# First sequence's difference-attention value pages issued by SyncE instead of GpSimd

## The chip, the core and the metric

The kernel runs on one core of a Trainium2 chip. The time is that of one execution on the device in microseconds (us), and the median of three runs of the kernel before is 1414.11 us. The core has five engines that run their own instruction streams and meet at semaphores: TensorE (PE in the profile), VectorE (DVE), ScalarE (ACT), GpSimd (POOL) and SyncE (SP). SyncE and GpSimd issue nearly all transfers of this kernel.

## The reference, cut to what matters

One decoder layer works on a prompt of 256 tokens and on 8 sequences of 8 new tokens each, all with one set of weights. The part in question is the attention of the 8 new-token sequences over 1024 cached positions. It has a sparse mixer and a difference mixer:

```python
def diff_attention(q, k, v, qp, kp, lam):
    ...
        s = jnp.einsum('bqhcd,bkhcd->bhcqk', q_b, k) * SCALE
        p = masked_softmax(s, kp[None, :] <= qp_b[:, None])
        p_diff = p[:, :, 0] - lam * p[:, :, 1]
        return jnp.einsum('bhqk,bkhe->bqhe', p_diff.astype(v.dtype), v)
```

The cached keys and values lie in pages of 128 positions, picked by a page table. Each sequence has 8 pages of difference keys (`cache_diff_k`, 256 KB each), 8 of difference values (`cache_diff_v`, 256 KB each), 8 of compressed keys and values (`cache_cmp_kv`, 128 KB each) and 8 of selected ones (`cache_sel_kv`, 128 KB each). After the attention come two projections and a mixture of 32 experts.

## The kernel before, in words

The cached attention runs in four turns, each for a pair of sequences, b = 0 and b = 1 (`PAIRS_OF_SEQ` is 4). The first three turns are a hardware loop on each engine and the fourth is written out. Every engine follows an order written out by hand, and semaphores join them. No scheduler decides anything.

TensorE's turn, in the order of the code (`turn` in `pe_attention`):

- `kd0` to `kd7` (L611) transpose the key pages of this turn's b = 1 out of `dk_raw`, spread among the matmuls of `hidden` (L625). Then come the difference scores (L634, L639).
- A second run of `hidden` follows, with `pd0` to `pd2` and the groups of selected and window keys among it, then the scores of the sparse mixer (L749 to L757).
- `dif_values(0)` multiplies the b = 0 probabilities with `dv_raw[0]` (L687, L689), then a small product (L766), then `dif_values(1)` does the same with `dv_raw[1]`. Each adds one to the semaphore `l_pv`. These two are called D0 and D1 below.
- `nk0` and `nk1` (L611) then transpose the first key pages of the next turn's b = 0. Before `nk0` TensorE waits until four pages (0 to 3) have landed in `dk_raw`, and before `nk4` until pages 4 to 7 have. `ps0`, `ps1`, a product (L776), `pw` and `pm` lie between, and `nk2` to `nk7` follow.
- The values of the sparse mixer (L701 to L708) and the next turn's b = 0 scores (L634) end the turn.

There is one `dk_raw` for all keys, so it is filled twice per turn: with the pages of b = 0 of turn i during turn i - 1, as `kd0` to `kd7` of that turn free it, and with those of b = 1 as `nk0` to `nk7` free it. `dv_raw` has a buffer for each b.

SyncE issues, for each turn, the keys of b = 0 (`dk_pages(i, 0)`, which waits for `kd3` and `kd7` of turn i - 1), the keys of b = 1 (`dk_pages(i, 1)`, which waits for `nk3` and `nk7`), and the selected pages (`sel_pages`, which wait for the last values of the turn). A read of the page table (`pages_of`, L465) stands at the head of each pass.

GpSimd issues the compressed pages (`cmp_pages`, L482, which wait for VectorE's `cmp_turned`), copies queries (L545), and issues the value pages of both sequences (`values_in`, L539). Those of b = 0 wait until D0 of the turn before has read the old ones, and those of b = 1 until D1 of the turn before and `pd2` of the present turn are over.

An instruction that waits holds up all that stand behind it on its engine.

Of the kernel before, what the change touches and what calls it, by code (L numbers as in the profile page):

```python
# [30 lines left out]
NPAGE = PAST // PAGE  # L31
RUN = 4
# [119 lines left out]
def build(nc, io, const_a, at_a, const_b, at_b):  # L152
    ctx = ExitStack()
    with ctx:
# [4 lines left out]
        def at(off, *dims):  # L159

            n = int(np.prod(dims))
            v = arena[:, off:off + n]
            if len(dims) == 2:
                return v.rearrange("p (a b) -> p a b", b=dims[1])
            if len(dims) == 3:
                return v.rearrange("p (a b c) -> p a b c", b=dims[1], c=dims[2])
            if len(dims) == 4:
                return v.rearrange("p (a b c d) -> p a b c d", b=dims[1], c=dims[2], d=dims[3])
            return v
# [9 lines left out]
        dv_raw = [at(6144, NPAGE, 512), at(33792, NPAGE, 512)]  # L179
# [102 lines left out]
        pv_full, nsa_out, dif_out = sem("pv_full"), sem("nsa_out"), sem("dif_out")  # L282
# [16 lines left out]
        STAGES = (("sel", 0), ("win", 0), ("cmp", 0), ("dif", 0), ("dif", 1), ("sel", 1), ("win", 1), ("cmp", 1))  # L299
# [90 lines left out]
        dv_in = [sem(f"dv_in{k}") for k in range(4)]  # L390
        l_tp, l_out = sem("l_tp"), [sem("l_out_act"), sem("l_out_dve")]
# [5 lines left out]
        l_pv, l_osm = sem("l_pv"), sem("l_osm")  # L397
# [4 lines left out]
        def past(eng, s, n):  # L402


            eng.wait_ge(s, n + 1)
# [14 lines left out]
        SCORES, EXPS, VALUES = 2, 4, 3  # L420
        SC_DIF, SC_NSA = 1, 2
        EXP_DIF, EXP_CMP, EXP_SEL, EXP_WIN = 1, 2, 3, 4
        PV_D0, PV_D1, PV_NSA = 1, 2, 3
# [9 lines left out]
        def group_at(name, final=False):  # L433
            return (LAST_GROUPS if final else LOOP_GROUPS).index(name)
# [28 lines left out]
        def pages_of(engine, i, b):  # L463

            return nc.values_load_multi_w_load_instructions(ptab[0:1, bass.ds(i * (2 * NPAGE) + b * NPAGE, NPAGE)], engines=(engine,),  # L465
                                                            min_val=0, max_val=NPOOL - 1, skip_runtime_bounds_check_because=PAGES_ARE_OF_THE_POOL)[1]

        def in_runs(raw, quad, h):

            return raw[h::RUN, RUN * quad:RUN * quad + RUN, :]  # L470

        def page_runs(pool_d, page):

            return pool_d[bass.ds(page, 1)].rearrange("a (p r) n -> (a p) r n", r=RUN)
# [10 lines left out]
        def win_pages(eng, i):  # L485

            win_d = io["state_win_kv"][0].rearrange("n p c g d -> n p (c g d)")
            for b in range(2):
                eng.dma_start(win_raw[:, b], win_d[bass.ds(2 * i + b, 1)].rearrange("a (p r) n -> (a p) r n", r=RUN)).then_inc(win_in[b], 16)

        def sync_attention(sp, early):

            flat = lambda name: io[name][0].rearrange("n p c g d -> n p (c g d)")
            sel_d = flat("cache_sel_kv")
            kd_d = io["cache_diff_k"][0].rearrange("n p h c d -> n p (h c d)")
            def sel_pages(i, pages, first=False):
                if not first:
                    past(sp, l_pv, i * VALUES)
                for b in range(2):
                    for k in range(2):  # L500
                        for h in range(4):
                            sp.dma_start(in_runs(sel_raw[:, b], k, h), page_runs(sel_d, pages[b][4 * k + h])).then_inc(sel_in[2 * b + k], 16)

            def dk_pages(i, b, pages, first=False):

                for pg, page in enumerate(pages):
                    if pg % RUN == 0:
                        if first and b:
                            past(sp, l_tp, pg + RUN)
                        elif not first:  # L510
                            past(sp, l_tp, i * L_TP + (NPAGE - L_TP + group_at(f"nk{pg + RUN - 1}" if b else f"kd{pg + RUN - 1}") + 1))
                    sp.dma_start(in_runs(dk_raw, pg // RUN, pg % RUN), page_runs(kd_d, page)).then_inc(dk_in[pg // 4], 16)

            if early:
                out_done(sp, G_QK + 14)
                dk_pages(0, 0, pages_of(SP, 0, 0), True)
                return
            pages = [pages_of(SP, 0, b) for b in range(2)]
            sp.wait_ge(gate_full, 9)
            sel_pages(0, pages, True)  # L520
            dk_pages(0, 1, pages[1], True)
            sp.wait_ge(gate_full, 12)
            win_pages(sp, 0)
            past(sp, l_sc, SC_DIF)
            with sp.Fori(1, PAIRS_OF_SEQ) as i:
                pages = [pages_of(SP, i, b) for b in range(2)]
                dk_pages(i, 0, pages[0])
                dk_pages(i, 1, pages[1])
                sel_pages(i, pages)
            sync_merge(sp)  # L530

        def pool_attention(pool, st):
            vd_d = io["cache_diff_v"][0].rearrange("n p h e -> n p (h e)")

            def values_in(pages, i, b, first=False):
                for pg, page in enumerate(pages):
                    if pg == 0 and not first:
                        past(pool, l_pv, i * VALUES + ((PV_D1 if b else PV_D0) - VALUES))
                    pool.dma_start(in_runs(dv_raw[b], pg // RUN, pg % RUN), page_runs(vd_d, page)).then_inc(dv_in[2 * b + pg // 4], 16)  # L539

            def queries_of(i, first=False):
                if not first:
                    past(pool, l_sc, i * SCORES)
                for src, dst in ((bd_raw, cur_raw), (bd_rot, cur_rot), (bd_dif, cur_dif)):
                    nc.gpsimd.tensor_copy(dst, src[:, bass.ds(2 * i, 2), :]).then_inc(l_cur, 1)  # L545

            arrived(pool, "small")
            out_done(pool, G_QK + 14)
            queries_of(0, True)
            pages = [pages_of(POOL, 0, b) for b in range(2)]  # L550
            for n in range(12):
                j, t = gate_unit(n)
                c0 = 2 * D * t + 512 * (j - 6)
                if n == 5:
                    pool.wait_ge(ph_full, 2)
                    cmp_pages(pool, pages[0], 0, 0, first=True)
                if n == 8:
                    cmp_pages(pool, pages[1], 0, 1, first=True)
                pool.wait_ge(gate_out, n + 1)
                if t < 2:  # L560
                    pool.dma_start(gate_pre[:, c0:c0 + 512], gate_stage[n % 2]).then_inc(gate_stored[n % 2], 16)
                else:
                    for h in range(2):
                        pool.dma_start(gate_pre[0:NS, c0 + 256 * h:c0 + 256 * h + 256], gate_stage[n % 2][64 * h:64 * h + 64, 0:256]).then_inc(gate_stored[n % 2], 16)
            pool.wait_ge(pv_full, len(STAGES))
            past(pool, l_tp, NPAGE + group_at("kd0") + 1)
            values_in(pages[0], 0, 0, True)
            for n in (10, 11):
                gates_stored(pool, n)
            pool.wait_ge(stored, n_stored)  # L570
            cmp_pages(pool, pages_of(POOL, 1, 0), 1, 0)
            values_in(pages[1], 0, 1, True)

            def next_turn(i, last):

                pages = [pages_of(POOL, i, b) for b in range(2)]
                cmp_pages(pool, pages[1], i, 1, range(4))
                queries_of(i)
                cmp_pages(pool, pages[1], i, 1, range(4, NPAGE))
                values_in(pages[0], i, 0)  # L580
                if not last:
                    cmp_pages(pool, pages_of(POOL, i + 1, 0), i + 1, 0)
                if last:
                    pool.wait_ge(l_hid, 2 * PAIRS_OF_SEQ - 1)
                    nsa_weights(pool, 1, 0)
                past(pool, l_tp, i * L_TP + (NPAGE + group_at("pd2", last) + 1))
                values_in(pages[1], i, 1)
                if last:
                    pool.wait_ge(l_hid, 2 * PAIRS_OF_SEQ)
                    pool.wait_ge(dv_in[2], 64 * PAIRS_OF_SEQ)  # L590
                    nsa_weights(pool, 1, 1)

            with pool.Fori(1, PAIRS_OF_SEQ - 1) as i:
                next_turn(i, False)
            next_turn(PAIRS_OF_SEQ - 1, True)
            pool_moe(pool, st)

# [2173 lines left out]
```

## Time and profile before

| | |
|---|---|
| median of three runs | 1414.11 us (1413.07 to 1416.83) |
| the profiled execution's own time | 1414.01 us |
| its span | 1412.3 us |
| TensorE busy | 1376.0 us, 97% of the span |
| VectorE, ScalarE, GpSimd busy | 467.8, 285.5 and 99.1 us |
| mean granted clock of TensorE | 0.999 |
| value pages issued by GpSimd | 64, median 5.3 us from issue to landing |
| difference key pages issued by SyncE | 64, median 6.2 us from issue to landing |

The span is what the trace covers. The execution's own time is 1.7 us longer. Busy time leaves out the instructions that only issue a transfer, move a register or wait. All starts given below are in us from the start of the span.

### The profile page before, as it was taken

To read this page: it belongs to the slowest core of one execution; us is meant where nothing else is said; L and a number is where in the kernel's file an instruction comes from. 1 tells how busy PE (TensorE), PEld (TensorE's weight loads), DVE (VectorE), ACT (ScalarE), POOL (GpSimd) and SP (SyncE) were. 2 spreads that over 40 slices of the span, in tenths; PEclk is the share of its full clock that TensorE was granted. 3 is DMA by queue.
4 is the path that set the end of the run, shared out by engine and by line. 5 is a ranking of instruction groups with operands and counts; after the bars stand their busy time and mean duration, and the time that the engine had idled before them with its cause. 6 is when DMAs were issued, how large, how long until landed. Compare 5 with 4: busy or idle time off the path is not lost.

```text
span 1412.3 us, 19613 instructions
## 1 busy us (share of the span) xinstructions
PE 1376.0 (97%) x7357; PEld 602.8 (43%) x7357; DVE 467.8 (33%) x1025; ACT 285.5 (20%) x611; POOL 99.1 (7%) x220
## 2 busy tenths in 40 slices
PE   9999999999999999999999999999999999999987
PEld 4445556777754543333333333333333333333322
DVE  1115484665436442313313223132121331321314
ACT  2004434555540301001101010000101111001002
POOL 1000223434200000000000000000000000000000
PEclk9999999999999999999999999999999999999999
DMA  7335857999987699999999999999999999999996
GB/s 274 119 119 197 290 127 244 325 288 311 354 273 308 280 426 396 421 430 428 429 428 430 427 429 428 428 428 429 428 428 429 428 427 430 428 428 428 429 428 247
DMA packets 75516, 509.39 MB, mean 361 GB/s; under 512 B 19114, under 2 KB 25746, under 8 KB 46130
## 3 DMA queue, kind: packets, MB, share of 16 engines
q1 hardware_dynamic: 60978, 476.30, 82.8%
q0 software_dynamic: 13472, 28.87, 6.5%
q10 hardware_dynamic: 1024, 3.67, 0.7%
q8 instruction: 25, 0.41, 0.1%
q14 instruction: 17, 0.14, 0.0%
HBM read 502.29 MB, written 10.62 MB: 363 GB/s over the span
## 4 chain that ended last, share of the span: by engine, by line
PE 79%; DMA 16%; issue 2%; ACT 2%; DVE 1%; SPq 0%; POOL 0%; POOLq 0%; DVEq 0%; ACTq 0%
PE PS L1505 25%; PE PS L1535 11%; DMA arena<-in_w_gate_up 10%; PE PS L1475 6%; PE PS L365 5%; DMA arena<-in_w_down 5%; PE PS L2224 4%; PE PS L1467 4%; PE PS L625 3%; PE PS L611 3%; PE PS L1362 2%; PE PS L1174 2%; PE PS L377 1%; PE PS L2189 1%; PE PS L1522 1%
## 5 line engine op out<-in xcount | busy, mean ns | idle before, releaser
L1505 PE MATMUL PS<-arena 128*64 128x512 f32 x2048 | 455.8, 595 | 12.3 <-DMA arena<-in_w_gate_up 12.2
L1505 PEld LDWEIGHTS PS<-arena 128*64 128x64 f32 x2048 | 141.7, 137 | 293.6 <-issue 263.7
L1535 PE MATMUL PS<-arena 128*64 128x512 f32 x1024 | 227.0, 594 | 2.4 <-DMA arena<-in_w_down 2.3
L1969 DVE TENSOR_SCALAR arena<-PS 128x512 f32<-128x512 f32 x32 | 22.1, 692 | 444.0 <-PE PS L1514 443.0
L1535 PEld LDWEIGHTS PS<-arena 128*64 128x64 f32 x1024 | 71.7, 137 | 150.1 <-issue 143.7
L1475 PE MATMUL PS<-arena 128*128 128x512 f32 (+1 forms) x180 | 84.2, 608 | 0.0
L1467 PE MATMUL PS<-arena 128*128 128x512 f32 (+1 forms) x192 | 79.4, 618 | 4.5 <-ACT arena L1675 3.6
L1886 DVE TENSOR_TENSOR arena<-PS,arena 128x512 f32<-128x512 f32 (+1 forms) x33 | 22.0, 672 | 167.2 <-PE PS L1483 166.7
L365 PE MATMUL PS<-arena 128*128 128x512 f32 (+1 forms) x192 | 77.0, 562 | 0.0
L1323 POOL COPY arena<-arena 96x64 bf16 (+1 forms) x34 | 7.9, 233 | 985.4 <-PE PS L1542 940.3
L1660 ACT ACTIVATE arena<-arena 128x512 f32<-128x512 f32 x32 | 20.1, 630 | 266.3 <-DVE arena L1969 266.3
L1667 ACT ACTIVATE arena<-PS 128x512 f32<-128x512 f32 x32 | 19.1, 597 | 251.5 <-PE PS L1522 251.5
L625 PE MATMUL PS<-arena 128*128 128x252 f32 x256 | 68.1, 382 | 0.0
L611 PE MATMUL PS<-arena 128*128 128x128 f32 (+1 forms) x456 | 65.6, 277 | 1.0 <-DMA arena<-in_cache_diff_k 0.7
L1674 ACT ACTIVATE arena<-PS 64x512 f32<-64x512 f32 x31 | 18.3, 589 | 222.9 <-PE PS L1542 222.9
L2224 PE MATMUL PS<-arena 128*128 128x512 f32 x128 | 59.9, 601 | 0.0
L611 PEld LDWEIGHTS PS<-arena 128*128 128x128 f32 (+1 forms) x456 | 53.1, 141 | 15.5 <-issue 5.4
L881 ACT ACTIVATE arena<-PS 128x512 f32<-128x512 f32 (+5 forms) x96 | 44.7, 491 | 59.4 <-PE PS L611 57.4
L365 PEld LDWEIGHTS PS<-arena 128*128 128x128 f32 x192 | 36.2, 190 | 40.0 <-issue 38.4
L1475 PEld LDWEIGHTS PS<-arena 128*128 128x128 f32 (+1 forms) x180 | 31.6, 188 | 46.0 <-issue 45.9
L625 PEld LDWEIGHTS PS<-arena 128*128 128x128 f32 x256 | 42.7, 190 | 4.6 <-issue 1.5
L1467 PEld LDWEIGHTS PS<-arena 128*128 128x128 f32 (+1 forms) x192 | 24.9, 171 | 43.8 <-issue 36.9
(297 smaller groups left out, 1272.7 us busy)
## 6 DMA issues: line engine op xcount, KB each, us to landing
arena<-in_w_gate_up SPq DMA_DIRECT2D x128, 2048.0 KB, 20.0
arena<-in_w_down SPq DMA_DIRECT2D x62, 2048.0 KB, 21.8
arena<-in_cache_diff_k SPq DMA_DIRECT2D x64, 256.0 KB, 6.2
arena<-in_cache_diff_v POOLq DMA_DIRECT2D x64, 256.0 KB, 5.3
arena<-in_w_in SPq DMA_DIRECT2D x7, 2048.0 KB, 12.6
arena<-in_cache_cmp_kv POOLq DMA_DIRECT2D x64, 128.0 KB, 4.0
arena<-in_cache_sel_kv SPq DMA_DIRECT2D x64, 128.0 KB, 6.9
arena<-in_w_out SPq DMA_DIRECT2D x1, 4096.0 KB, 14.3
```

The source lines that it names most:

```text
L365: last = nc.tensor.matmul(bank(proj_bank(q, 2 * s + t))[:, 0:w], xnT[:, k, 128 * t:128 * t + 128], chunk_at(j)[:, k, 0:w], start=(k == 0), ...
L611: last = nc.tensor.transpose(place[0:c, col:col + r], src, ident[0:r, 0:r])
L625: last = nc.tensor.matmul(hidden_at[c], w1[:, c, l, :], cmp_window(c, l), start=(l == 0), stop=(l == CB // 2 - 1))
L881: copy = lambda d, s: nc.scalar.activation(d, s, ACT.Copy)
L1174: last = nc.tensor.matmul(bank(BRANCH_BANK[v][half])[p:p + r], src[:, k, 128 * t:128 * t + r], w[:, k, 512 * nh:512 * nh + 512], start=(k ...
L1362: last = nc.tensor.matmul(bank(Z_BANK[v])[p:p + r], mT[:, k, 128 * t:128 * t + r], w_out[:, k, 512 * nh:512 * nh + 512], start=(k == 0), s ...
L1467: last = nc.tensor.matmul(out, spread[:, 128 * t:128 * t + ROWS[t]], ypair[:, 512 * h:512 * h + 512], start=True, stop=True)
L1475: last = nc.tensor.matmul(bank(h), pick[0:ROWS[t], t], hn[t][0:ROWS[t], 512 * h:512 * h + 512], start=(t == 0), stop=(t == 2))
L1505: last = nc.tensor.matmul(bank(2 + role + 2 * u)[64 * h:64 * h + 64], hTm[:, k, BS * u:BS * u + BS], rows[:, D * role + 512 * h:D * role + ...
L1535: last = nc.tensor.matmul(bank(6 + u)[64 * h:64 * h + 64], aT[u][:, c % 4, 64 * (c // 4):64 * (c // 4) + 64], down_w[u][c // 4][:, c % 4, ...
L1969: st(V.tensor_scalar(g1, bank(2 + 2 * u), LIM, None, ALU.min), g1_ready)
L2224: last = nc.tensor.matmul(bank(7), xnT[:, k, 128 * t:128 * t + 128], chunk_at(j)[:, k], start=(k == 0), stop=(k == KD - 1))
```

## The change

The helper `values_in` of GpSimd becomes `value_pages(eng, ...)`, which any engine can call. SyncE calls it for b = 0: for turn 0 behind the window pages, with the two waits that GpSimd had there, and for turns 1 to 3 at the head of the pass, ahead of `dk_pages(i, 0)`. GpSimd keeps the value pages of b = 1 and no longer issues those of b = 0. The wait of each b = 0 group for D0 of the turn before goes with it to SyncE. No buffer, no size and nothing on TensorE, VectorE or ScalarE is changed.

```diff
+        def value_pages(eng, pages, i, b, first=False):
+
+            vd_d = io["cache_diff_v"][0].rearrange("n p h e -> n p (h e)")
+            for pg, page in enumerate(pages):
+                if pg == 0 and not first:
+                    past(eng, l_pv, i * VALUES + ((PV_D1 if b else PV_D0) - VALUES))
+                eng.dma_start(in_runs(dv_raw[b], pg // RUN, pg % RUN), page_runs(vd_d, page)).then_inc(dv_in[2 * b + pg // 4], 16)
+
...
             win_pages(sp, 0)
+            sp.wait_ge(pv_full, len(STAGES))
+            past(sp, l_tp, NPAGE + group_at("kd0") + 1)
+            value_pages(sp, pages[0], 0, 0, True)
             past(sp, l_sc, SC_DIF)
             with sp.Fori(1, PAIRS_OF_SEQ) as i:
                 pages = [pages_of(SP, i, b) for b in range(2)]
+                value_pages(sp, pages[0], i, 0)
                 dk_pages(i, 0, pages[0])
                 dk_pages(i, 1, pages[1])
                 sel_pages(i, pages)
...
             past(pool, l_tp, NPAGE + group_at("kd0") + 1)
-            values_in(pages[0], 0, 0, True)
             for n in (10, 11):
                 gates_stored(pool, n)
             pool.wait_ge(stored, n_stored)
             cmp_pages(pool, pages_of(POOL, 1, 0), 1, 0)
-            values_in(pages[1], 0, 1, True)
+            value_pages(pool, pages[1], 0, 1, True)
...
                 cmp_pages(pool, pages[1], i, 1, range(4, NPAGE))
-                values_in(pages[0], i, 0)
                 if not last:
                     cmp_pages(pool, pages_of(POOL, i + 1, 0), i + 1, 0)
...
                 past(pool, l_tp, i * L_TP + (NPAGE + group_at("pd2", last) + 1))
-                values_in(pages[1], i, 1)
+                value_pages(pool, pages[1], i, 1)
```

On SyncE, at the head of the loop pass, the order before is this. The L465 rows read the page table, and an `ISA` row works out a register for the transfer behind it.

```order
L489 DMA arena<-in_state_win_kv 128x1024
L525 UNCONDITIONAL_BRANCH [waits l_sc]
L525 ISA
L465 TENSOR_LOAD arena
L465 ISA
L465 TENSOR_LOAD arena
L405 ISA
L512 ISA [waits l_tp]
L512 DMA arena<-in_cache_diff_k 32x2048
```

The first transfer of a pass is a key page of b = 0. It waits for `l_tp`, TensorE's count of transposed groups.

On SyncE, at the same place, the order of the changed kernel is this (L536 is the loop, L497 the value pages).

```order
L536 UNCONDITIONAL_BRANCH [waits l_sc]
L536 ISA
L465 TENSOR_LOAD arena
L465 ISA
L465 TENSOR_LOAD arena
L405 ISA
L497 ISA [waits l_pv]
L497 DMA arena<-in_cache_diff_v 32x2048
```

The pass now begins with a wait for `l_pv`, which is D0 of the turn before. Seven more value pages follow it. The end of that group and the key pages of b = 0 (L520 now) read so:

```order
L497 DMA arena<-in_cache_diff_v 32x2048
L405 ISA
L520 DMA arena<-in_cache_diff_k 32x2048 [waits l_tp]
L520 DMA arena<-in_cache_diff_k 32x2048 x3
L405 REGISTER_ALU
L520 DMA arena<-in_cache_diff_k 32x2048 [waits l_tp]
L520 DMA arena<-in_cache_diff_k 32x2048 x3
L405 REGISTER_ALU
L520 ISA [waits l_tp]
```

All key pages of a pass stand behind the wait for `l_pv` and the eight value pages. The eight key pages of b = 0 follow one another without an `ISA` row between them.

On GpSimd, between the second half of the compressed pages of b = 1 and those of the next turn, the order before has the wait for `l_pv` at the head of eight value pages.

```order
L482 ISA
L482 DMA arena<-in_cache_cmp_kv 32x1x1024
L405 ISA
L539 ISA [waits l_pv]
L539 DMA arena<-in_cache_diff_v 32x2048
```

In the changed kernel the compressed pages of the next turn follow at once.

```order
L482 ISA
L482 DMA arena<-in_cache_cmp_kv 32x1x1024
L465 ISA
L465 TENSOR_LOAD arena
L481 ISA
L482 ISA [waits cmp_turned]
L482 DMA arena<-in_cache_cmp_kv 32x1x1024
```

The wait that stands there now is the one for `cmp_turned`, VectorE's count of turned compressed pages.

## Rows read from the trace of the kernel before

**Rows 1.** The page, busy time by engine (share of the span, instructions).

```profile
PE 1376.0 (97%) x7357; PEld 602.8 (43%) x7357; DVE 467.8 (33%) x1025; ACT 285.5 (20%) x611; POOL 99.1 (7%) x220
```

**Rows 2.** The waits of TensorE: who for whom, us in total, times, longest.

```profile
PE PS L1505 <- DMA arena<-in_w_gate_up: 12.2, 17, 1.3
PE PS L1467 <- ACT arena L1675: 3.6, 14, 0.3
...
PE PS L687 <- DMA arena<-in_cache_diff_v: 1.1, 1, 1.1
...
PE PS L611 <- DMA arena<-in_cache_diff_k: 0.7, 1, 0.7
```

**Rows 3.** The timeline of TensorE, turn 0: start us, us, line, operation, count.

```profile
260.00 0.42 PE L689 MATMUL PS<-arena 64*32 64x128 f32 x8
...
262.84 0.42 PE L689 MATMUL PS<-arena 64*32 64x128 f32 x8
263.19 2.33 PE L611 MATMUL PS<-arena 128*128 128x128 f32 x16
265.36 0.39 PE L776 MATMUL PS<-arena 128*128 128x128 f32 x2
265.73 3.87 PE L611 MATMUL PS<-arena 128*128 128x128 f32 x31
```

**Rows 4.** The timeline of TensorE, turns 1 and 2, and into turn 3.

```profile
303.12 0.42 PE L689 MATMUL PS<-arena 64*32 64x128 f32 x8
...
307.44 2.00 PE L611 MATMUL PS<-arena 128*128 128x128 f32 x16
...
347.18 0.42 PE L689 MATMUL PS<-arena 64*32 64x128 f32 x8
...
350.55 2.19 PE L611 MATMUL PS<-arena 128*128 128x128 f32 x16
...
364.55 0.65 PE L611 MATMUL PS<-arena 128*128 128x128 f32 x4 [0.73 <-DMA arena<-in_cache_diff_k]
```

**Rows 5.** The timeline of SyncE's queue over the turns.

```profile
227.07 5.05 SPq L512 DMA_DIRECT2D arena<-in_cache_diff_k  x8
232.16 1.06 SPq L489 DMA_DIRECT2D arena<-in_state_win_kv  x2
247.73 25.61 SPq L512 DMA_DIRECT2D arena<-in_cache_diff_k  x16
273.62 11.27 SPq L502 DMA_DIRECT2D arena<-in_cache_sel_kv  x16
```

**Rows 6.** Key pages from issue to landing, all 64.

```profile
DMA to landing us min/median/max: 2.8/6.2/8.9
```

**Rows 7.** Key pages from issue to landing, the eight issued from 247 to 253 us.

```profile
DMA to landing us min/median/max: 6.1/7.9/8.9
```

**Rows 8.** The timeline of GpSimd, turns 0 and 1.

```profile
258.19 2.33 POOL L482 DMA_DIRECT2D arena<-in_cache_cmp_kv  x4 [7.75 <-DVE arena L863]
260.51 0.87 POOL L545 COPY arena<-arena 128x128 f32 x3
261.45 2.32 POOL L482 DMA_DIRECT2D arena<-in_cache_cmp_kv  x4
263.87 4.57 POOL L539 DMA_DIRECT2D arena<-in_cache_diff_v  x8
274.89 4.67 POOL L482 DMA_DIRECT2D arena<-in_cache_cmp_kv  x8 [6.46 <-DVE arena L863]
```

**Rows 9.** Windows: us, PE, PEld, DVE, ACT, POOL busy, PEclk, DMA share, GB/s.

```profile
253.00:257.00 4.00, 4.00 (x29) 2.51 (x29) 3.46 (x5) 2.82 (x6) 0.00 (x0) 1.00 1.00 418
261.00:265.00 4.00, 3.90 (x86) 3.21 (x86) 3.39 (x8) 2.72 (x6) 3.73 (x8) 1.00 0.69 179
```

**Rows 10.** Windows after TensorE's last matmul (same columns).

```profile
1408.00:1409.00 1.00, 0.00 (x0) 0.00 (x0) 0.98 (x1) 0.00 (x0) 0.00 (x0) 0.80 0.93 307
1409.00:1412.00 3.00, 0.00 (x0) 0.00 (x0) 0.30 (x1) 0.00 (x0) 0.00 (x0) 0.50 0.66 268
```

**Rows 11.** The timeline of TensorE at the start and at the end of the span.

```profile
1.62 4.43 PE L2200 MATMUL PS<-arena 128*128 128x512 f32 x6 [1.62 <-DVE arena L2583]
...
10.89 27.73 PE L365 MATMUL PS<-arena 128*128 128x512 f32 x64
...
1398.76 4.71 PE L1467 MATMUL PS<-arena 128*64 128x512 f32 x12 [0.86 <-DVE arena L2037]
```

More of the change, by code:

```diff
@@ L532, in pool_attention @@
         def pool_attention(pool, st):
[L533 to L539, printed above, removed]
             def queries_of(i, first=False):
```

## The prediction

> **What bounds the kernel now.** I read the page first. TensorE is busy 1376.0 of 1412.3 us [rows 1], so only about 36 us of the span are free of matmuls, and whatever makes TensorE stand still lengthens the kernel nearly one for one. Next I read the waits of TensorE alone [rows 2]. The reader is to see how little a better placed transfer can win. In the cached attention TensorE waited 1.1 us for value pages (once, before D1 of turn 1) and 0.7 us for key pages (once, before `kd0` of turn 3). The 12.2 us for expert weights lie much later and have nothing to do with this part. The value pages of b = 0, which are the ones that move, made nobody wait. A change of their issue can therefore win some 1.8 us at most, 0.13% of the time.
>
> Third, the timeline of TensorE around D0, D1 and `nk0`, once per turn. In turn 0 D0 ends at 260.00 + 0.42 = 260.42 and `nk0`, the first L611 behind D1, starts at 263.19 [rows 3]: 2.8 us later. In turn 1 the two are 303.54 and 307.44, 3.9 us apart with the 1.1 us wait in between. In turn 2 they are 347.60 and 350.55, 2.95 us apart [rows 4]. Fourth, the timeline of SyncE's queue [rows 5]. The key pages that `nk0` of turn 0 needs (keys of b = 0 of turn 1) are issued from 247.73 on, 15.5 us ahead of their use. SyncE could do that because its only waits there (`kd3`, `kd7`) were long over. All 16 key pages of the pass are in that row because the eight of b = 1 stand behind the first eight and wait for `nk3`.
>
> **The change part by part.** *Removed from GpSimd:* 4 groups of 8 value pages, 4.57 us of issuing each [rows 8]. GpSimd is no bound: behind the group at 263.87 it stood idle 6.46 us for VectorE's L863, and the next compressed pages started at 274.89. They wait for the same L863 afterwards. Gain on TensorE: nothing.
>
> *Turn 0's value pages on SyncE:* the two window pages are issued from 232.16 for 1.06 us, and the next thing SyncE did was at 247.73 [rows 5]. Eight issues take about 5.1 us (eight key pages took 5.05), so they fit into that gap. They are used by D0 some 2.3 us before 260.42. Cost nothing. If the gap were not there, `dk_pages` of turn 1 would slip by 5 us, and that is overruled by the next point anyway.
>
> *The wait at the head of each pass.* This is the whole case. SyncE now stands at the wait for D0 of the turn before, and behind it are queued the eight value pages, the eight key pages of b = 0, those of b = 1 and the selected pages. For the key pages of b = 0 it is too late, because TensorE wants the first four 2.8 us after D0. For turn 0:
>
> - D0 ends at 260.42. I allow 0.3 us for SyncE to wake up (no row shows it; at 0 the stall is that much shorter), so the first value page is issued at 260.7.
> - Eight value pages at the pitch of key pages, 5.05 / 8 = 0.63 us with the register work (x16 selected pages: 11.27 / 16 = 0.70) [rows 5]. I take 0.65, so 5.2 us. The first key page is issued at 265.9.
> - `nk0` needs key pages 0 to 3. The fourth is issued 3 pitches later. The order shows these without register work between them, like the window pages at 0.53 us each [rows 5]. With 0.53 to 0.65 us that is 1.6 to 1.95 us, and I take 1.7. It is issued at 267.6.
> - From issue to landing: 2.8 to 8.9 us, median 6.2 [rows 6]. The eight issued while GpSimd issued value pages too took 6.1 to 8.9 [rows 7]. I take 6.4, a little above the median, because 12 pages of 256 KB come in a row (0.25 MB per 0.6 us is some 420 GB/s, and the DMA engines carried 418 GB/s at a share of 1.00) while in the stretch where this begins they had only been busy to 0.69 [rows 9]. Landed at 274.0.
> - `nk0` starts at 274.0 instead of 263.2: a stall of 10.8 us, 13.6 us after D0.
>
> Turn 1: 303.54 + 13.6 = 317.1 against 307.44, 9.7 us. It is less because the old 1.1 us wait lies inside the new one. Turn 2: 347.60 + 13.6 = 361.2 against 350.55, 10.65 us. Turn 3 has no `nk` groups and its own pages come in turn 2's pass. The sum of the three is 31.2 us. By the ends of [rows 6] it is 3 x 3.6 us less (20.4) or 3 x 2.5 us more (38.7).
>
> *What is late next.* `nk4` wants pages 4 to 7. The eighth is issued at most 2.6 us behind the fourth, and `nk4` comes about 4.4 us behind `nk0`: from 263.19 to 265.73, then 15 of the 31 transposes of 3.87 us [rows 3]. No second stall. The keys of b = 1 are issued behind `nk3` and used at `kd0`, both of which move along with `nk0`. So do the selected pages. The distance between them stays, with fewer transfers beside them, so the 0.73 us wait at 364.55 [rows 4] should go: 0.7 us back.
>
> *The clock.* TensorE's last matmul ended at 1398.76 + 4.71 = 1403.5 [rows 11]. The granted clock was 0.80 on average in the window from 1408 to 1409 and 0.50, which is 1.2 GHz, behind it [rows 10]. So it fell at 1408.6, about 5.1 us after the last matmul. A stall of 10 us is longer. After it TensorE starts slowly, as at the start of the span: there six matmuls took 4.43 us, where 64 of the same size took 27.73 us later, 0.433 each [rows 11]. Six at that pace would be 2.6 us, so a cold start cost 1.8 us. (The record of the granted clock shows no low level there, only the durations do.) I count 1.5 us per stall, because behind `nk0` the copies out of the transposed banks also set the pace. Bounds 0 and 1.8. The sum is 4.5 us, with ends 0 and 5.5.
>
> The Trainium skill's page "TensorE: Matmul & The Clock Gate" (Part 1: The HAM clock gate) has the half rate as the default state, which activity lifts. By that rule the loss behind each stall is certain, and by the last rows of the trace it is likely. It changes the sum by the 4.5 us counted.
>
> **Sum.** 31.2 + 4.5 - 0.7 = 35.0 us. The profiled execution took 1414.01 us, 0.1 us below the median, so the forecast is 1449.0 us, 2.5% slower. None of it comes back later. The expert weights wait for the branch products behind the attention, and transfers ahead of them were not what TensorE waited for. The ends are 1414.0 + 20.4 - 0.7 = 1433.7 and 1414.0 + 38.7 + 5.5 = 1458.2.
>
> **The rivals.**
>
> *A, the same stalls but more of them.* The half-speed stretch and the burst push the keys of b = 1 and the selected pages so that `kd0` or a group of selected keys waits as well. The wait of 0.73 us at 364.55 shows that this distance has no reserve. A further 4 us in each turn gives 1449 + 12 = 1461. Against it: everything there is issued relative to `nk3`, and competing value pages have gone from that stretch.
>
> *B, the burst lands fast.* When SyncE stands at the wait, no other transfers but some compressed pages are under way. The shortest landing in the trace was 2.8 us, and the clock may not fall in a stall of 7 us. That gives 1433.7. Against it: the 12th page of a burst is not the first.
>
> *C, not slower.* The key pages are hidden anyway. For this the first four would have to be down 2.8 us after D0. That decides it: with SyncE released before about 251 (263.2 less 6.4 less 5.2 less 0.3), nothing is lost, the two waits of [rows 2] can go, and the time is 1414.0 - 1.8 = 1412.2. It would be so if the wait were satisfied by the turn before the last one. By the code it is not: it asks for a count that D0 of the turn before gives. In turn 0 that is 260.4.
>
> The Trainium skill's page "DMA: Bandwidth & Descriptors" (Issuing engines are not separate DMA queues) says that transfers from SyncE, ScalarE and GpSimd run on the same 16 DMA engines and interleave. Read alone, with equal landing times (medians of 5.3 us for GpSimd's value pages and 6.2 us for SyncE's key pages in this trace), that speaks for C: who issues does not matter. It says nothing of what waits behind the issue on the same engine, and that is where the cost is.
>
> *D, faster by more than the measurement can tell.* About 0.3% (4 us) is what can be told from no change. The waits in this part sum to 1.8 us, so there is nothing to win it from.
>
> **How the numbers follow.** Forecast 0.78, A 0.09, B 0.07, C 0.04, D 0.02. The likeliest is 1449. To leave out no more than 2 in 10 the range covers the forecast's own spread, about 3 us of landing time either way at two or three stalls and the clock's ends, and part of B and A: 1438 to 1460. Slower by over 0.3%: 0.78 + 0.09 + 0.07 = 0.94. Within 0.3%: 0.04. Faster: 0.02.
>
> **What the profile of the changed kernel would show.** TensorE's waits: L611 for `in_cache_diff_k`, three times, 9 to 11 us each, before `nk0` of turns 0, 1 and 2, where now no such wait is. SyncE's own waits: the value pages for TensorE's L689, three times. Key pages of b = 0 issued about 5.5 us after D0 in each turn, and the 12 pages from the first value page on in some 7 us. A granted clock under 1.00 behind each stall. GpSimd with fewer issues and more idle time, and the experts' part of the same length, only later. I am wrong if L611 doesn't wait there, if `kd0` or the selected groups wait as long as `nk0`, or if the experts' part gets shorter.

## The result, and the profile after

| | before | changed |
|---|---|---|
| median of 4 runs each | 1414.79 us (1413.07 to 1416.83) | 1456.53 us (1453.93 to 1460.98) |
| ratio | | 1.0295, 95% interval 1.0276 to 1.0314 |
| profiled execution, its span | 1414.01, 1412.3 us | 1456.32, 1454.4 us |
| mean granted clock | 0.999 | 0.984 |

The change makes the kernel 2.95% slower. The forecast was 1449.0 us, with a range of 1438 to 1460. The span grew by 42.1 us.

The waits of TensorE in the changed kernel (who for whom, us in total, times, longest):

```profile
PE PS L613 <- DMA arena<-in_cache_diff_k: 37.9, 3, 12.8
PE PS L1507 <- DMA arena<-in_w_gate_up: 12.3, 17, 1.3
PE PS L1469 <- ACT arena L1677: 3.6, 14, 0.3
...
PE PS L1176 <- DMA arena<-in_w_br_nsa: 1.7, 1, 1.7
...
PE PS L689 <- DMA arena<-in_cache_diff_v: 0.7, 1, 0.7
```

The line that was 0.7 us in [rows 2] is now 37.9 us in three waits, all of them before `nk0`; the old wait at `kd0` of turn 3 is gone. The waits of the experts' part (L1507, L1469) are as before. From its L1469 at 606.46 to the last one at 1440.75 it takes 834.3 us, and from 564.51 to 1398.76 it was the same before. Lines of the attention are numbered 2 higher than before (L613 was L611, L691 was L689).

The timeline of TensorE around the three waits, in turns 0, 1 and 2. These rows answer to [rows 3, 4].

```profile
259.71 0.42 PE L691 MATMUL PS<-arena 64*32 64x128 f32 x8
...
275.75 3.68 PE L613 MATMUL PS<-arena 128*128 128x128 f32 x16 [12.78 <-DMA arena<-in_cache_diff_k]
...
317.83 0.42 PE L691 MATMUL PS<-arena 64*32 64x128 f32 x8
...
333.59 3.35 PE L613 MATMUL PS<-arena 128*128 128x128 f32 x16 [12.50 <-DMA arena<-in_cache_diff_k]
...
340.91 0.65 PE L703 MATMUL PS<-arena 128*32 128x64 f32 x32
...
374.37 0.42 PE L691 MATMUL PS<-arena 64*32 64x128 f32 x8
...
390.23 3.67 PE L613 MATMUL PS<-arena 128*128 128x128 f32 x16 [12.59 <-DMA arena<-in_cache_diff_k]
```

From the end of D0 to `nk0` it is now 15.6, 15.3 and 15.4 us (before 2.8, 3.9 and 2.95). The chain of waits shows of what the 15.3 us of turn 1 are made. It lists pieces in order of time: start, us, what. `SPq` is an instruction of SyncE that issues a transfer, L497 for value pages and L520 for key pages.

```profile
317.90 0.40 PE PS L691 x8
318.45 0.49 SPq L497
...
323.37 0.47 SPq L497
...
324.03 0.47 SPq L520
324.59 0.54 SPq L520
325.23 0.55 SPq L520
325.87 7.67 DMA arena<-in_cache_diff_k
333.59 3.35 PE PS L613 x16
```

D0 ends at 318.25, SyncE issues its first value page 0.2 us later, the first key page after another 5.6 us, the fourth 1.85 us behind the first, and this one lands 7.7 us later. Each of these steps lay on the chain in all three turns, and the landings of the fourth key page took 7.3, 7.7 and 7.7 us.

The queue of SyncE in the changed kernel, which answers to [rows 5]. The first row holds the value pages of turn 0, the wait for D0, and those of turn 1.

```profile
234.09 32.27 SPq L497 DMA_DIRECT2D arena<-in_cache_diff_v  x16
266.54 22.21 SPq L520 DMA_DIRECT2D arena<-in_cache_diff_k  x16
289.00 12.45 SPq L510 DMA_DIRECT2D arena<-in_cache_sel_kv  x16
```

Key pages that were issued from 247.73 on are now issued from 266.54 on. The clock fell in each stall. Windows of the changed kernel, the first five in turn 0, two in turn 1, two in turn 2 (columns as in [rows 9]):

```profile
263.00:267.00 4.00, 0.00 (x0) 0.00 (x0) 0.70 (x2) 1.05 (x4) 0.28 (x1) 0.72 1.00 280
...
274.00:275.00 1.00, 0.00 (x0) 0.00 (x0) 0.00 (x0) 0.00 (x0) 0.00 (x0) 0.50 1.01 418
...
279.00:280.00 1.00, 1.00 (x7) 1.00 (x6) 0.11 (x1) 0.74 (x2) 0.00 (x0) 0.50 0.00 0
280.00:282.00 2.00, 2.00 (x12) 1.96 (x11) 0.80 (x5) 0.95 (x4) 0.00 (x0) 0.54 0.02 4
282.00:284.00 2.00, 2.00 (x19) 1.82 (x18) 1.58 (x8) 1.61 (x4) 0.00 (x0) 1.00 0.00 0
...
326.00:327.00 1.00, 0.00 (x0) 0.00 (x0) 0.00 (x0) 0.00 (x0) 0.00 (x0) 0.61 1.08 303
...
336.00:337.00 1.00, 1.00 (x8) 0.97 (x7) 0.28 (x1) 0.56 (x2) 0.00 (x0) 0.77 0.00 0
...
378.00:382.00 4.00, 0.00 (x0) 0.00 (x0) 0.40 (x2) 0.71 (x3) 0.00 (x0) 0.86 1.00 266
...
394.00:395.00 1.00, 1.00 (x9) 1.00 (x9) 0.29 (x1) 0.59 (x2) 0.00 (x0) 0.75 0.00 0
```

A mean of 0.72 over 4 us with levels of 1.00 and 0.50 puts the fall at 264.8, 1.8 us after the last matmul of D1, and 0.54 puts the rise at 281.8, 6.1 us after `nk0` began. The other turns differ: by the same working the clock fell 5.1 us after D1 in turn 1 and 3.3 us after it in turn 2, and rose 2.9 and 4.3 us after `nk0` began. From `nk0` to the sparse values (L703) the changed kernel took 8.6, 7.3 and 7.8 us where the kernel before took 6.3, 6.0 and 6.2: 5.2 us in all, and the most in turn 0, where the clock came back latest.

The account: 37.9 us of waits for keys, less 1.1 us that turn 1 had waited for value pages, less the 0.7 us at `kd0` of turn 3 (gone, as forecast), plus 5.2 us of slow pace. Two small waits grew in turn 3 and right behind it, by 0.7 us for value pages and by 0.8 us for `w_br_nsa`. That is 42.8 us, against 42.1 measured. D0 of turn 0 also began 0.3 us earlier.

### The profile page after: what moved, and what is told of

Its sections match the earlier page's. It is cut to its first block, busy times and chain, and to the rows that moved or that the text cites. A ratio compares the mean times of both kernels' runs of the same rounds, so it can differ in the third digit from the quotient of the medians.

```text
span 1454.4 us, 19588 instructions
## 1 busy us (share of the span) xinstructions
PE 1380.6 (95%) x7357; PEld 609.2 (42%) x7357; DVE 467.4 (32%) x1025; ACT 285.9 (20%) x611; POOL 82.2 (6%) x188
## 4 chain that ended last, share of the span: by engine, by line
PE 78%; DMA 17%; SPq 1%; ACT 1%; issue 1%; DVE 1%; POOLq 0%; POOL 0%; DVEq 0%
PE PS L1507 25%; PE PS L1537 11%; DMA arena<-in_w_gate_up 10%; PE PS L1477 6%; PE PS L365 5%; DMA arena<-in_w_down 5%; PE PS L627 4%; PE PS L613 4%; PE PS L2226 4%; PE PS L1469 4%; PE PS L1364 2%; PE PS L1176 2%; DMA arena<-in_cache_diff_k 2%; PE PS L377 1%; PE PS L2191 1%
## 5 line engine op out<-in xcount | busy, mean ns | idle before, releaser
L1507 PE MATMUL PS<-arena 128*64 128x512 f32 x2048 | 455.8, 595 | 12.4 <-DMA arena<-in_w_gate_up 12.3
L1507 PEld LDWEIGHTS PS<-arena 128*64 128x64 f32 x2048 | 141.6, 137 | 293.8 <-issue 263.8
L613 PE MATMUL PS<-arena 128*128 128x128 f32 (+1 forms) x456 | 70.7, 294 | 37.9 <-DMA arena<-in_cache_diff_k 37.9
L1469 PE MATMUL PS<-arena 128*128 128x512 f32 (+1 forms) x192 | 79.4, 618 | 4.5 <-ACT arena L1677 3.6
L613 PEld LDWEIGHTS PS<-arena 128*128 128x128 f32 (+1 forms) x456 | 59.6, 152 | 50.7 <-DMA arena<-in_cache_diff_k 38.7
L1477 PEld LDWEIGHTS PS<-arena 128*128 128x128 f32 (+1 forms) x180 | 31.6, 188 | 46.0 <-issue 45.9
L1469 PEld LDWEIGHTS PS<-arena 128*128 128x128 f32 (+1 forms) x192 | 24.9, 171 | 43.8 <-issue 36.9
```

The costliest lines, as they stand in the source:

```text
L613: last = nc.tensor.transpose(place[0:c, col:col + r], src, ident[0:r, 0:r])
L1469: last = nc.tensor.matmul(out, spread[:, 128 * t:128 * t + ROWS[t]], ypair[:, 512 * h:512 * h + 512], start=True, stop=True)
L1477: last = nc.tensor.matmul(bank(h), pick[0:ROWS[t], t], hn[t][0:ROWS[t], 512 * h:512 * h + 512], start=(t == 0), stop=(t == 2))
L1507: last = nc.tensor.matmul(bank(2 + role + 2 * u)[64 * h:64 * h + 64], hTm[:, k, BS * u:BS * u + BS], rows[:, D * role + 512 * h:D * role + ...
```

## The experiments

Each ratio is against runs of the kernel before on the same chip. Theory Q was that SyncE's queue behind the wait for D0 is the whole cost. The theories against it are named in each expectation.

**keys_first.** Only the order of two lines is changed.

```diff
-                value_pages(sp, pages[0], i, 0)
                 dk_pages(i, 0, pages[0])
+                value_pages(sp, pages[0], i, 0)
                 dk_pages(i, 1, pages[1])
```

> The changed kernel with two lines swapped: in each pass SyncE issues the eight key pages of b = 0 first and the value pages of b = 0 (with their wait for D0) behind them. GpSimd still doesn't issue them. Theory Q (the queue behind the wait): only what stands behind the wait for D0 is late, and of that only the keys of b = 0 are wanted soon. They are out again before D0, the three stalls of 12.5 to 12.8 us at nk0 go, the clock stays at 1.00, and the time is that of the kernel before within 0.3%: 1411 to 1417 us. The keys of b = 1 stand behind the eight value pages, which are out 5.5 us after D0, before nk3 is over (7 us after D0), so they lose nothing. Theory M (the move itself costs: value pages of 256 KB on SyncE's queue beside the keys there slow the keys down): the time stays above 1435 us, with waits for keys at nk0 or kd0.

Measured: 1422.76 us against 1415.30, ratio 1.0049 (1.0031 to 1.0067). 82% of the loss went (34.3 of 41.7 us), and with it, in the profiled execution, every wait for keys. What is left lies outside the range of theory Q, and also far under theory M's. In the profiled execution (1417.7 us, the shortest of the six) TensorE waited 5.5 us in three waits for VectorE, which had waited for compressed pages. The waits of TensorE, then one of VectorE's own from 255 to 400 us:

```profile
PE PS L613 <- DVE arena L1054: 5.5, 3, 2.0
```

```profile
DVE arena L865 <- DMA arena<-in_cache_cmp_kv: 9.9, 3, 3.4
```

GpSimd issues the second half of the compressed pages at 261.21 there, 0.9 us behind SyncE's first value page (260.35). From issue to landing they took 5.2, 6.9 and 10.1 us (least, median, most). In the kernel before they took 2.6, 3.2 and 4.1, and there GpSimd issued the value pages behind them, from 263.87 on [rows 8]. So the move costs something by itself, though not where theory M put it. The profiled execution shows 3.7 us of it (5.5 us of these waits, less the 1.8 us of waits in [rows 2] that are gone). The other five executions took 1418.5 to 1425.6 us and left no trace, so what the rest of the median's 7.5 us is made of isn't shown.

**wait_only.** The kernel before, with the wait alone.

```diff
+                past(sp, l_pv, i * VALUES + (PV_D0 - VALUES))
                 dk_pages(i, 0, pages[0])
```

> The kernel before with one line added: SyncE waits for D0 of the turn before at the head of each pass, ahead of the keys of b = 0. GpSimd issues all value pages as before. Theory Q: the keys' first page is issued about 0.3 us after D0 instead of 6 us, the fourth 2 us later, and it lands 6 to 7 us behind that: 9 us after D0 instead of 15.6. Each stall at nk0 is 6 to 7 us instead of 12.6, and with 1.3 to 2.2 us of slow pace behind it the time is 1414.8 + 3 x 8 = 1439 us (1434 to 1444). Theory T (traffic: what makes the keys late is the burst on the DMA engines, the wait costs little by itself): the keys meet only compressed pages and the value pages that GpSimd issues 3 us later, and the time is under 1428 us.

Measured: 1440.04 us, ratio 1.0176 (1.0156 to 1.0196). The waits of TensorE:

```profile
PE PS L612 <- DMA arena<-in_cache_diff_k: 19.0, 3, 6.7
```

That is 6.3 us a stall, and the time is about 1 us above theory Q's. The wait by itself, with not one transfer moved to another engine, makes 59% of the loss (24.7 of 41.7 us). Theory T is out as the whole cause.

**half_pages.** Value pages 0 to 3 of b = 0 go out on SyncE, 4 to 7 on GpSimd, in turn 0 as well, which the diff leaves out.

```diff
-                value_pages(sp, pages[0], i, 0)
+                value_pages(sp, pages[0], i, 0, these=range(4))
...
                 cmp_pages(pool, pages[1], i, 1, range(4, NPAGE))
+                value_pages(pool, pages[0], i, 0, these=range(4, NPAGE))
```

> The changed kernel with the value pages of b = 0 split: SyncE issues pages 0 to 3 (behind the wait for D0, ahead of the keys), GpSimd pages 4 to 7 at its old place. Theory Q: four issues fewer are ahead of the keys, 2.6 to 2.8 us, and each stall at nk0 is 9.8 to 10.2 us instead of 12.6: 1456.5 - 8 = 1448.5 us (1446 to 1451). It lies half way between the run with the wait alone and the changed kernel. Theory T: the same 2 MB of values go over the same DMA engines in the same stretch, only from two queues, so the keys land no sooner: 1453 to 1458 us.

Measured: 1450.49 us, ratio 1.0248 (1.0229 to 1.0268). The time is in theory Q's range and outside theory T's, but the stalls were 11.8, 10.6 and 10.7 us, where theory Q had 9.8 to 10.2. Four issues fewer ahead of the keys saved 1.6 us a stall on average and not 2.7. The chain shows why: the first key page did go out sooner (in turn 1 2.6 us behind the first value page instead of 5.6), but the first four key pages came out more slowly (2.5 us instead of 1.85 there), and the fourth took 8.8, 8.1 and 8.7 us to land instead of 7.3, 7.7 and 7.7. GpSimd issued its four value pages at just that time (266.35 to 268.62 in turn 0, where the keys went out from 265.70).

**quarter_bytes.** Each value page of b = 0 in turns 1 to 3 brings a quarter of its columns. The kernel leaves out the rest, so what it computes is not the layer.

```diff
-                value_pages(sp, pages[0], i, 0)
+                value_pages(sp, pages[0], i, 0, cols=128)
...
-                eng.dma_start(in_runs(dv_raw[b], pg // RUN, pg % RUN), page_runs(vd_d, page)).then_inc(...)
+                eng.dma_start(in_runs(dv_raw[b], pg // RUN, pg % RUN)[:, :, 0:cols], page_runs(vd_d, page)[:, :, 0:cols]).then_inc(...)
```

> The changed kernel, but of each value page of b = 0 in turns 1 to 3 only a quarter of the columns is loaded (64 KB instead of 256 KB), so D0 of these turns works on old values for the other heads. The number of issues and their order are those of the changed kernel. Theory Q, with the time on SyncE's queue as the price of a page: the issues keep their pace of 0.65 us, the stall shortens only by what the keys waited inside the DMA engines (they took about 7.3 us from issue to landing, 6 would be usual), 1 to 1.5 us a stall: 1451 to 1455 us. Theory T: 1.5 MB less ahead of the keys, at some 0.42 MB per us, are 3.7 us a stall: 1443 to 1447 us.

Measured: 1446.83 us, ratio 1.0222 (1.0204 to 1.0241), in theory T's range and outside theory Q's. The issues kept their pace (eight value pages from 314.80, the first key page at 320.64). The landing of the keys changed. From issue to landing of the eight key pages of one group (issued from 324.03 in the changed kernel and from 320.64 in this one), the changed kernel first:

```profile
DMA to landing us min/median/max: 6.8/7.0/7.7
```

```profile
DMA to landing us min/median/max: 3.0/4.1/4.6
```

The stalls were 10.0, 9.1 and 9.3 us. So of a stall's 12.6 us about 3.2 us are keys that queue inside the DMA engines because of 1.5 MB of values, and that I had not expected. It is not a price that adds to the queue's, because the keys had company in wait_only too: there the fourth key page took 6.6, 6.8 and 7.3 us to land with no value page ahead of it (GpSimd issued eight from 263.75 on, 3 us behind the first key page), and 4.0, 4.0 and 4.3 us here. The stalls of the changed kernel are 6.3 us longer than those of wait_only, which is 5.6 us of value pages on SyncE's queue and 0.7 us of landing.

**filler** and **filler_short.** Matmuls whose result nobody uses fill the stall, so that TensorE is busy in it. `filler` has 100 and outlasted the stall. The diff is that of `filler_short`, with 50. In the trace each of them counts as two instructions.

```diff
                 dif_values(1)
+                if not final:
+                    place = group_place(i, group_at("nk0"), final)
+                    for _ in range(50):
+                        nc.tensor.matmul(place[:, 0:64], ident, kwT[:, 0:64], start=True, stop=True)
                 group("nk0")
```

> The changed kernel with 100 small matmuls more (identity times 64 columns, into the bank that nk0 overwrites) between D1 and nk0 in turns 0 to 2. They fill some 11 of the 12.6 us in which TensorE waits for keys and compute nothing that is used. Theory C (the clock falls in the stall, and this makes the work behind it slow): the granted clock stays at 1.00, the stretch from nk0 to the sparse values takes 6.0 to 6.3 us as in the kernel before instead of 7.3 to 8.6, and the time is 5 us shorter than the changed kernel's: 1451.5 us (1449.5 to 1453.5). Rival (the work behind the stall is slow because the copies out of the banks have to start up again, whatever the clock): the stretch stays at 7.3 us or more and the time at 1455 us or more.

> The changed kernel with 50 small matmuls more (identity times 64 columns, into the bank that nk0 overwrites) between D1 and nk0 in turns 0 to 2. In the run filler 100 of them took 22.5 us and outlasted the stall, so 50 take 11.3 of the 12.6 us in which TensorE waits for keys. They compute nothing that is used. Theory C (the clock falls in the stall, and this makes the work behind it slow): the granted clock stays at 1.00, the stretch from nk0 to the sparse values takes 6.0 to 6.3 us as in the kernel before instead of 7.3 to 8.6, and the time is 5 us shorter than the changed kernel's: 1451.5 us (1449.5 to 1453.5). Rival (the work behind the stall is slow because the copies out of the banks have to start up again, whatever the clock): the stretch stays at 7.3 us or more and the time at 1455 us or more.

Measured for `filler`: 1479.61 us, ratio 1.0458 (1.0435 to 1.0481). The 100 matmuls took 22.5 us a turn, so its time says nothing on the question, but it shows the stretch from `nk0` to L703 at 5.97 us in turn 0, with a clock of 1.00.

Measured for `filler_short`: 1451.74 us, ratio 1.0255 (1.0227 to 1.0283), which is 4.8 us below the changed kernel's median, as theory C said (5.2 us if each is taken against the kernel before of its own session). Its timeline of TensorE in turns 0 and 2 (L775 is the filler), and a window in turn 2:

```profile
262.68 11.38 PE L775 MATMUL PS<-arena 128*128 128x64 f32 x100
275.80 2.00 PE L613 MATMUL PS<-arena 128*128 128x128 f32 x16 [1.74 <-DMA arena<-in_cache_diff_k]
...
281.82 0.65 PE L703 MATMUL PS<-arena 128*32 128x64 f32 x32
...
386.39 2.83 PE L613 MATMUL PS<-arena 128*128 128x128 f32 x16 [1.87 <-DMA arena<-in_cache_diff_k]
```

```profile
387.00:388.00 1.00, 1.00 (x9) 1.00 (x8) 0.45 (x1) 0.60 (x1) 0.00 (x0) 0.66 0.10 41
```

In turn 0 the 16 transposes took 2.00 us instead of 3.68, and `nk0` started at the same time (275.80 and 275.75). The stretch was 6.0 us in turns 0 and 1, with a granted clock of 1.00. In turn 2 theory C's 1.00 did not hold, and the stretch was 7.4 us: 1.9 us were left of the wait, and the clock fell at 387.3, 0.9 us after the transposes had begun. So of the 5.2 us of slow pace the three turns got back 2.6, 1.3 and 0.5 us. The slow pace follows the clock in both directions, and the rival, copies that have to start up again, would have left turn 0 at 7.3 us or more.

**values_after_d1.** keys_first, with the value pages held back until D1.

```diff
-                    past(eng, l_pv, i * VALUES + ((PV_D1 if b else PV_D0) - VALUES))
+                    past(eng, l_pv, i * VALUES + (PV_D1 - VALUES))
```

> The kernel of the run keys_first with the wait at the head of its value pages set one step later: SyncE issues the value pages of b = 0 only after D1 (2.8 us behind D0), when GpSimd has issued the second half of the compressed pages of b = 1. keys_first came out 0.5% slower than the kernel before, with VectorE waiting 3.3 us in each of three turns for compressed pages that landed after 6.9 us (median) instead of 3.2, and TensorE waiting 5.5 us in all for VectorE's L1054. Theory O (the old place behind the compressed pages on GpSimd's queue was an order that protected them; value pages issued at the same time on another queue slow them): the landing is back at 3 to 4.5 us, both waits go, and the time is that of the kernel before: 1413 to 1418 us. Rival (SyncE's queue or the later issue costs by itself): the keys of b = 1, which come right behind the values, land late and TensorE waits at kd0, 2 us a turn: 1421 to 1426 us.

Measured: 1419.74 us over 12 runs (1414.64 to 1423.69) against 1415.25 over 17, ratio 1.0028 (1.0014 to 1.0042). In the profiled execution theory O held: the compressed pages landed after 2.8, 3.2 and 4.6 us, the waits for L1054 and for compressed pages were gone, and its 1414.64 us is the kernel before. SyncE is still the one that issues the value pages, only from 263.45 on instead of 260.35. So it is enough for the compressed pages that the values are issued later; GpSimd's queue did this by its order. But that was the shortest execution of the twelve, and the median is above the range. Two more executions of the same kernel were profiled.

> A second look at the kernel of values_after_d1. Its profiled execution took 1414.6 us, but most others took 1418 to 1422 us with a mean granted clock of 0.995 to 0.998. If this execution is one of those, theory L (the keys of b = 1, issued 1.2 us later than in the kernel before, sometimes land too late) has TensorE waiting for keys at kd0, 1 to 3 us in some turn, with the clock falling behind it. The rival (chance in the experts' part, as the kernel before has executions of 1420 us too) has the attention as long as in the first look and the difference behind 560 us.

> A third look at the kernel of values_after_d1, with the same expectations as the second: a slower execution shows either more waiting for keys at kd0 within the attention (theory L) or a longer experts' part (the rival).

Measured: 1422.26 and 1420.65 us, one execution each, where the kernel before took 1413.91. Neither theory named the main place. TensorE waited for the value pages of b = 1, before D1, which GpSimd issues. The waits of TensorE in the second and in the third of these executions, and the longest of them in the third:

```profile
PE PS L689 <- DMA arena<-in_cache_diff_v: 4.7, 4, 2.5
```

```profile
PE PS L689 <- DMA arena<-in_cache_diff_v: 5.6, 3, 4.1
```

```profile
308.88 3.29 PE L689 MATMUL PS<-arena 128*32 128x128 f32 x64 [4.10 <-DMA arena<-in_cache_diff_v]
```

In the kernel before this wait is 1.1 us in one turn [rows 2], and in the first execution it is 1.3 us. The 64 matmuls behind the wait of 4.1 us took 3.3 us where they took 1.95 in the kernel before, with a granted clock of 0.55 from 309 to 312. Theory L's waits were there, but small: 1.0 us for keys of b = 1 in the first execution, 1.6 us in the second (0.3 at `kd0` and 1.3 at `kd4` of turn 1), none in the third, and 0.7 us in the kernel before. They don't tell the short execution from the long ones. In the third execution the eight value pages of turn 1 took 5.0, 7.2 and 10.2 us to land (least, median, most), against 5.5, 6.1 and 7.2 in the trace before. The experts' part is no longer, which puts the rival out: its first L1469 starts 7.4 and 6.1 us later than in the first execution, and the spans are 7.6 and 6.0 us longer. The place of the loss is shown. In the second the pages of turn 1 took no longer than in the kernel before (6.1 us median, 7.4 most), and those of turn 2 took up to 8.6 us. Why TensorE waits more for these pages in the long executions is open.

## Why the prediction was right

The forecast was 35.0 us more, and the span grew by 42.1. The mechanism, its three places and the two small gains were as stated. The size was not as good: the median is 7.5 us above the forecast and 4.5 us below the time of rival A, and only the rows, not the time, tell the two apart. Point by point:

- *What bounds the kernel.* Right. TensorE's new waits came through to the end one for one, and the experts' part neither shrank nor waited more.
- *GpSimd's part: gain nothing.* Right for the changed kernel. It was wrong as a statement on the move alone: keys_first shows that the old place also kept the value pages behind the compressed pages. In the changed kernel VectorE has no wait for compressed pages, because it reaches them only after TensorE's stall.
- *Turn 0's pages on SyncE: nothing.* Right, D0 of turn 0 started 0.3 us earlier.
- *The wait at the head of the pass.* Right in kind and too small: 31.2 us of stalls forecast, 37.9 measured. I had 13.6 us from D0 to `nk0`, and it was 15.3 to 15.6. Of the terms, in turn 1, waking took 0.2 us (0.3 forecast), eight value pages 5.6 us (5.2), three pitches 1.85 us (1.7), and landing 7.7 us (6.4). The mis-sized term is the landing. I took a value near the median of all key pages, although [rows 7], eight pages issued beside value pages, had 7.9. quarter_bytes shows that the bytes of the values are the cause. The argument that the DMA engines were only busy to 0.69 in the stretch where the burst begins does not hold, because the values themselves fill them before the keys come: their share was 1.00 from 263 to 267.
- *`nk4`, and the keys of b = 1.* No second stall, and the 0.7 us came back. Right.
- *The clock.* 4.5 us forecast, 5.2 measured, and 4.8 by the time of filler_short. It fell 1.8, 5.1 and 3.3 us after the last matmul, where the end of the span had shown 5.1, and stayed low for 6.1, 2.9 and 4.3 us of the work behind. The size was nearly right. The cost of a single stall was 2.3, 1.3 and 1.6 us, so that one of the three lay above the bound of 1.8. The Trainium skill's page "TensorE: Matmul & The Clock Gate" (Part 1: The HAM clock gate) has half rate as the default and activity as what lifts it. The rows agree: in each stall the clock went to 0.50 and came back behind it.
- *Rival A* (further stalls in each turn) had its time of 1461 within 5 us but not its mechanism: in the turns that it named there was no wait at `kd0` or at a selected group. *B, C and D* did not occur. In C the sum leaves out the 1.7 us of three pitches: SyncE would have to be released before 249.6, not 251. The upper end of 1458.2 leaves out the 0.7 us gain. Neither changes a chance.

## What to carry to other kernels

Before a transfer is moved to another engine because that one is free, list what stands behind it there: the wait that the transfer brings along holds up all of it, and here that was work wanted 2.8 us after the wait's own release. Then list what it stood behind where it was: that order may be what holds a large transfer back until a small, urgent one has landed. And size a landing by the rows with the same traffic ahead, not by the median of all.

## What was not expected of the hardware

- In one kernel, in three stalls of the same kind, the clock fell to 0.50 after 1.8, 5.1 and 3.3 us without a matmul, and came back after 6.1, 2.9 and 4.3 us of work. In filler_short it fell once 0.9 us after work had begun again behind a gap of 1.9 us (turn 2), and with a gap of 1.7 us in turn 0 it didn't.
- Key pages of the same size, issued at the same pace from the same queue, landed after 7.0 us (median) behind eight pages of 256 KB and after 4.1 us behind eight of 64 KB.
- Twelve executions of one kernel (values_after_d1) differed by 9 us (1414.6 to 1423.7), with a mean granted clock between 0.999 and 0.995. Two long ones that were profiled later waited 3.4 and 4.3 us more than the shortest for the value pages of b = 1.
